# Eight PSUM banks in turn for the paired products, and a later rearrangement of the residual on GpSimd

## The reference

```
h2 = rmsnorm(x, norm2_g);  x = x + (silu(h2 @ w_gate) * (h2 @ w_up)) @ w_down      # first block,  1024 -> 2816 -> 1024
h2 = rmsnorm(x, g_ffn);    x = x + square(relu(h2 @ w_ff1)) @ w_ff2                # second block, 1024 -> 4096 -> 1024
```

## Time and profile before

| | |
|---|---|
| median of 3 runs | 2442.06 us (2441.98 to 2444.38) |
| the profiled execution | 2445.13 us, span 2443.2 us |
| TensorE busy | 2388.4 us (98%), 11414 matmuls |
| VectorE / ScalarE / GpSimd busy | 1864.7 (76%) / 1090.2 (45%) / 1155.4 (47%) us |
| mean granted TensorE clock | 0.991 |

### The profile page before, as it was taken

How to read it: one execution, slowest core, us unless ns; L and a number is a source line. 1 busy time by engine, 2 the same in 40 slices (tenths; PEclk the granted TensorE clock), 3 DMA queues, 4 the chain that set the end, 5 groups by cost and what they waited for, 6 DMA issues and landing times.

```text
span 2443.2 us, 31864 instructions
## 1 busy us (share of the span) xinstructions
PE 2388.4 (98%) x11414; PEld 1958.1 (80%) x11414; DVE 1864.7 (76%) x2405; ACT 1090.2 (45%) x1868; POOL 1155.4 (47%) x786
## 2 busy tenths in 40 slices
PE   9999999999999999999999999999999999999998
PEld 7777788888778888878877878887877888788876
DVE  6777767673687787789967966778288888999976
ACT  6454556562533333344435436555163333544423
POOL 4666651211555555554543463431256555554552
PEclk9999999999999999999999999999999999999999
DMA  4311321232122233363512772223223444654522
GB/s 161 81 48 52 92 61 36 60 122 70 52 65 78 88 115 103 104 200 119 181 54 105 179 163 61 61 59 109 76 81 108 146 148 160 228 168 148 180 80 101
DMA packets 228171, 263.06 MB, mean 108 GB/s; under 512 B 18224, under 2 KB 139824, under 8 KB 227888
## 3 DMA queue, kind: packets, MB, share of 16 engines
q1 hardware_dynamic: 224416, 248.72, 32.0%
q0 software_dynamic: 3168, 11.54, 2.5%
q10 hardware_dynamic: 432, 0.79, 0.1%
HBM read 169.74 MB, written 60.82 MB: 94 GB/s over the span
## 4 chain that ended last, share of the span: by engine, by line
PE 81%; DVE 9%; POOL 3%; ACT 3%; issue 3%; DMA 1%; SPq 0%; POOLq 0%; DVEq 0%; ACTq 0%
PE PS L1810 23%; PE PS L1815 23%; PE PS L1812 23%; PE PS L1908 3%; PE PS L1895 2%; PE PS L1929 2%; PE PS L1926 2%; PE PS L1889 2%; DVE R L2292 1%; DVE R L2222 1%; ACT R L2580 1%; DVE R L2252 1%; PE PS L1892 1%; DVE X L2300 1%; DVE Pb L2114 0%
## 5 line engine op out<-in xcount | busy, mean ns | idle before, releaser
L1810 PE MATMUL PS<-R,wh 128*128 128x512 f32 x2872 | 1139.3, 397 | 23.6 <-DVE mix L2203 6.3
L2670 POOL TENSOR_TENSOR lows<-values,wh 128x512 fp32r<-128x512 f32 (+1 forms) x486 | 718.3, 1484 | 903.7 <-ACT wh L2421 730.0
L1815 PE MATMUL PS<-R,wh 128*128 128x512 f32 x2872 | 1124.8, 392 | 2.6 <-DVE R L2248 1.9
L1812 PE MATMUL PS<-R,lows 128*128 128x512 f32 x2564 | 1002.7, 391 | 1.2 <-POOL lows L2670 1.2
L1810 PEld LDWEIGHTS PS<-R,wh 128*128 128x128 f32 x2872 | 542.5, 189 | 136.1 <-DVE mix L2203 7.6
L1815 PEld LDWEIGHTS PS<-R,wh 128*128 128x128 f32 x2872 | 541.3, 188 | 122.2 <-DVE R L2248 3.7
L1812 PEld LDWEIGHTS PS<-R,lows 128*128 128x128 f32 x2564 | 483.3, 189 | 96.0 <-issue 3.6
L2421 ACT ACTIVATE wh<-values 128x512 fp32r<-128x512 f32 (+2 forms) x487 | 301.9, 620 | 578.9 <-PE PS L1815 575.4
L2300 DVE TENSOR_TENSOR X<-PS,X 128x1024 f32<-128x1024 f32 x154 | 187.2, 1216 | 31.1 <-PE PS L1815 30.5
L2670 POOL TENSOR_TENSOR late_r<-late,wh 128x512 fp32r<-128x512 f32 x77 | 114.0, 1480 | 118.3 <-ACT wh L2421 56.3
L2537 ACT ACTIVATE PT<-PS 128x512 fp32r<-128x512 f32 (+1 forms) x200 | 108.2, 553 | 90.9 <-PE PS L1908 84.2
(11 more groups left out here) (279 smaller groups left out, 3027.9 us busy)
## 6 DMA issues: line engine op xcount, KB each, us to landing
scr_hid<-R1f SPq DMA_DIRECT2D x160, 256.0 KB, 3.0
values<-w_in_dram SPq DMA_DIRECT2D x88, 256.0 KB, 2.7
R1f<-scr_hid SPq DMA_DIRECT2D x88, 256.0 KB, 3.6
R0f<-scr_hid SPq DMA_DIRECT2D x86, 256.0 KB, 3.8
values<-w_ff_dram SPq DMA_DIRECT2D x60, 256.0 KB, 2.9
values<-w_ff_dram SPq DMA_DIRECT2D x100, 128.0 KB, 2.3
R<-R SPq DMA_DIRECT2D x96, 128.0 KB, 2.3
X<-X POOLq DMA_DIRECT2D x22, 512.0 KB, 5.8
```

Source lines behind the costliest of these rows:

```text
L1810: e.matmul(PS[:, b, :], wh, high, start=s["start"], stop=False, skip_group_check=on)
L1812: e.matmul(PS[:, b, :], wl, high, start=False, stop=False, skip_group_check=on)
L1815: m = e.matmul(PS[:, b, :], wh, low, start=False, stop=s["stop"], skip_group_check=on)
L2670: e.tensor_tensor(T.wl[piece.v][:, 0:m], T.wv[piece.v][:, 0:m], T.wh[:, piece.h, 0:m].bitcast(F), ALU.subtract).then_inc(*sg.up("w_lo", pi ...
```

## The change

Three things in the straight tiles and pairs. The straight tiles take all eight banks in turn. The pairs take the eight banks in the order of `SEVEN_BANKS`, which is 0, 1, 4, 5, 6, 7, 2, 3, starting at an index chosen so that the last product of the last pair is at the list's end. And `block_in` additionally waits for P4 of the pair before it in the list, the sixth and the eighth pair. A side effect: the line that set `dense_at` to 3 (n2) and 5 (n3) after the straight tiles is gone, so `dense_at` goes on from 8.

```
-            b = dict(P7=0, P4=1).get(name, self.seven_at % 3) if sums_late else self.seven_at % 3
+            b = SEVEN_BANKS[self.seven_at % 8]
...
-        O.dense_banks, O.dense_at = [2, 3, 0, 1], 0
+        O.dense_banks, O.dense_at = [2, 3, 0, 1, 4, 5, 6, 7], 0
...
-        O.dense_banks, O.dense_at = SEVEN_BANKS, -7 * len(factors) % 8
+        O.seven_at = -7 * len(factors) % 8
...
-                O.step("block_in", tag=tag, g=BLOCK_IN.index(i), given=whole)
+                O.step("block_in", tag=tag, g=BLOCK_IN.index(i), given=whole + [("dense", ((tag, i - 1), "P4"))])
```

## The result

| | before | changed |
|---|---|---|
| median | 2442.02 us (2441.25 to 2444.38, 4 runs) | 2413.01 us (2411.34 to 2416.88, 4 runs) |
| profiled execution, span | 2445.13, 2443.2 us | 2412.89, 2411.1 us |
| TensorE idle in the span | 54.8 us | 35.5 us |
| mean granted clock | 0.991 | 0.997 |

The ratio is 0.9882, 95% interval 0.9866 to 0.9897: 29.0 us faster. I had forecast 22.3 us and a range that ended at 2416.5. So the direction was right and the five places of my sum nearly so, and the size was too small by 6.7 us, outside the range.

A forecast was written before the change was run, and what follows sets the result against it. TensorE bounds the kernel, busy 2388.4 of 2443.2 us, so only its idling and clock loss can be won. Terms 8.4+0.8+3.0+0.6+4.7+3.5+1.3 = 22.3 us off 2442.06 give 2419.8, stated as 2420.0; range 2416.5 to 2428.

The forecast's parts named there:

- the five places of my sum: Gains: n2 start 8.4+0.8, n2 pairs' end 3.0, n3 start 0.6+4.7, n3 pairs' end 3.5, down projection 1.3 us.
- five clock stretches: At the seams: long stalls each bring a stretch at 1.2 GHz costing 1.7 us more; five fewer were expected.
- The coincidences of bank numbers: First pairs: with three banks, n2's pair 1 P1 stalls 0.79, n3's P7 3.04+1.7 clock; eight banks win 0.8+4.7.
- n3's P1: n3's first pair: P1 still takes the last straight half's bank; wait 0.9 in place of 1.52, 0.6 us won.
- The down projection: n3's direct tiles start at bank 6 instead of 3, where the last block's P5 just ended: 1.3 us won.
- The rearrangement costs nothing in the pairs: Behind P4 of the sixth and eighth pairs: cost 0, lows 1.2 us to spare; bounds 0 to +3.7 per place.
- The tiles between (projections with eight banks): Projections between the feed-forward stages and n3's direct tiles: banks turned by 5 of 8, gain nothing.
- a share returned: Pairs' ends: 3.6 (n2) and 4.2 (n3) won, 0.6 and 0.7 returned since VectorE's queue delays P6: 3.0 and 3.5.
- the first rival: Blocks after the pairs: they inherit the wait through VectorE's backlog, the 3.0 and 3.5 vanish, 2426.5 us; chance 0.10.
- The second: In the pairs: rearrangement makes lows or weight sums 2 us late at one to four places, +3.7 to +14.8; chance 0.12.
- The slower one: In the pairs: GpSimd waits for P4 a full product or more, lows late, 2441.8 to 2452.6 us; chance 0.03.
- The third: First pair: VectorE's own backlog, not banks, delays P6's right-hand sums, 9.2 us lost, 2429; chance 0.04.

The follow-up runs named there:

- e1: The kernel before with only the later rearrangement (block_in also waits for P4), banks as before: 2430.3 us against 2441.9.
- e8: The changed kernel with the pairs in three banks as before, the rest of the change in: 2425.8 us.
- e6: The kernel before with only dense_at set to 8 after the straight tiles in both stages: 2439.9 us against 2441.2.
- e10: The changed kernel with all four rearrangement instructions in one step behind P4 of the sixth pair: 2426.3 us.
- e5: The changed kernel with dense_at set to 3 and 5 after the straight tiles, as before: 2416.5 us.
- e9: The kernel of e5 with every engine's order planned for three pair banks and four straight-tile banks, late rearrangement in both plans: 2423.6 us.
- e3: The kernel before with eight banks for straight tiles and pairs, but engine orders planned for the old banks; rearrangement and dense_at as before: 2430.5 us.
- e2: The changed kernel without the later rearrangement, all bank edits in: 2421.95 us against 2441.9 for the kernel before.
- e12: The kernel before with eight planner passes in place of three, banks and rearrangement as before: 2432.5 us against 2443.1.

## Why the prediction was too small

**The step that failed.** My sum priced the waits next to the edited code and put everything else at nothing, as if each engine kept its order. It also gave back 0.6 and 0.7 us at the pairs' ends. In the profiled executions the places that I had at nothing gave 7.2 us, and nothing came back at the pairs' ends. TensorE's idle time fell by 19.3 us, where my sum has 13.8 (22.3 less five clock stretches, 8.5). The lower clock gave 12.8, where my sum has 8.5. For the whole change the mechanism at the five places was right, though at the pairs' ends and at n3's first seam the order has a share that I gave to the banks. What the sum lacked is the planner's new order and the clock stretches elsewhere. In the medians, where the clock's part is smaller, the miss is 6.7 us.

**Right, step by step.** GpSimd's rearrangement held VectorE at the n2 seam, and its move alone frees 8.5 us there (e1; 8.4 in my sum). The coincidences of bank numbers are gone with eight banks. With three, 0.78 is there in full, but the 3.04 has become 2.08 and 1.61 without a clock stretch (e1, e8), and 1.60 in e6, where the rearrangement stands at the seam. So a part of that term hung on the order. n3's P1 still waits, 0.79 (0.9 taken). The down projection gives 1.4 (1.3 taken). The rearrangement costs nothing in the pairs, with 1.3 us of cover left (1.2 taken; e10). Pairs still run at 226 ns a matmul.

**Point by point wrong.**

1. "The tiles between (projections with eight banks) are turned by 5 of 8: nothing" was wrong. Undoing it costs 3.5 us in the median (e5). 1.4 of them are the down projection, which I had. In the convolution and second attention 1.2 us of idle time come back, and the rest of the difference there is clock. That stretch also moves by 2.7 us between e5 and e9, which have the same banks in it, and is not won in e8, which has the turned banks. So the term was not nothing, but the turned banks are not shown to be its cause.
2. I took every row away from the edit as fixed. It isn't: one planner lays out all engines, and the new banks changed its limits. With the same banks and the same place of the rearrangement the order is worth 7.1 us (e9 against e5). In the traces it is 1.9 us at n2's pairs' end, 3.9 at n3's, 0.5 at n2's blocks' end, 1.7 at the last norm and 2.0 at the beginning (most of it one clock stretch), less the 2.7 that e9 wins in the convolution and second attention. So the terms that I took with a share returned (3.0 of 3.6, 3.5 of 4.2) came out whole, 3.8 and 4.4. The 0.8 at the last norm, where a stall of 1.38 us is gone, stood in no term.
3. In n2, at the blocks' end, I had index 3 before and after and no gain. The rows of the kernel before there and in n3's blocks:

```profile
1239.60 0.50 PE L1810 MATMUL PS<-R,wh 128*128 128x512 f32 x1 [1.77 <-DVE X L2300]
...
2200.08 0.50 PE L1810 MATMUL PS<-R,wh 128*128 128x512 f32 x1 [1.16 <-DVE X L2300]
```

The idle time went from 1.77 to 1.22, and the low-clock stretch behind it went too: 1.9 us. In e1 a stall of 1.76 at the same place came without that stretch, so 1.4 of the 1.9 is the clock's and not the change's. The 1.16 us in n3's blocks don't follow the banks either: they are gone in e1, e3, e5 and after, and there in e2 and e6 (1.06).
4. The bound. I put the lower end at "all lost time won" of the seams, less 2 us for scatter. With the planner re-laying the whole kernel, idle time and clock stretches anywhere are in play; e12 changes nothing but the order and moves 10.6 us. The upper end does not follow from its words: the first rival and one late place are 2426.5 + 3.7 = 2430.2, and I wrote 2428. That played no part in the miss.
5. I forecast five clock stretches fewer. The five at the seams are gone, but others went too, at n2's blocks' end and in the convolution and second attention, and how many come varies between runs of one kernel. So a part of the miss is luck.

**The rivals.** The first (blocks inherit the wait, 2426.5) needed the old order: e3 and e9 show it. The second had 1.3 us of cover against it, and no row at L1812 stands in the pairs. The slower one fell: GpSimd waited at most 0.8 us for P4 before a rearrangement, where it needed a full product. The third fell too: no idle row stands in the first pairs but the 0.79 before n3's P1, so VectorE's right-hand sums were done in time.

**The rule of the Trainium skill** (SBUF — State Buffer, Who interferes with whom): the hold is the same wherever the rearrangement stands, as the rule says, and the rows at 827 agree. What it can't say is whether anyone waits: at the seam TensorE did, in the pairs it didn't.

## What to carry to other kernels

Where a planner makes the order of all engines, an edit of one resource must be priced in two parts: the waits that it touches, read from the rows, and a free term for the re-laid order. Here that term was 7 us, and it can be measured by giving the old order to the new resources. Stretches at the lower clock belong in a term of their own, with a spread. Work that holds another engine up is best put where that engine has idle time and the consumer has cover, in pieces shorter than the cover: 5.1 us was free, 10.7 us in one piece cost 6.1 a time. More banks than three were worth nothing in the steady pairs; the gain was at seams, where the next stage's first buffers coincided with the last stage's last.

## What the runs showed of the hardware that I had not expected

The lower clock did not follow from the length of a stall alone. Windows of e1 (first two) and e2 (last) around three stalls of TensorE: 1.90 us at 1078 brought the mean clock to 0.83, 2.08 at 1859 and 2.10 at 1843 left it at 1.00:

```profile
1077.00:1087.00 10.00, 8.92 (x32) 7.24 (x33) 8.29 (x11) 5.25 (x10) 3.61 (x3) 0.83 0.87 284
1857.00:1867.00 10.00, 8.04 (x35) 6.68 (x36) 7.19 (x9) 3.66 (x6) 4.40 (x4) 1.00 0.17 50
```

```profile
1841.00:1851.00 10.00, 7.91 (x35) 6.56 (x36) 8.23 (x7) 4.06 (x7) 9.92 (x6) 1.00 0.40 138
```

The stall of 3.04 us at n3's first seam brought a stretch in the kernel before (0.83 in the earlier trace rows). In e12 it has the same length, at 1865.74, and none:

```profile
1863.00:1873.00 10.00, 7.25 (x32) 6.00 (x33) 7.98 (x10) 2.85 (x5) 4.14 (x4) 1.00 0.10 29
```

So the 1.7 us that I added to stalls above 1.8 is a price that some of them pay, not a term that each has; five stretches before and none after at the seams was as forecast.

GpSimd is slowed by VectorE as well. In the changed kernel the low parts with no SBUF-only instruction of VectorE beside them (under 5% of their time) take 1.31 us in the mean (119 of them), the others 1.46; in the kernel before 1.32 and 1.56. In e10 two of them take 1.27 at 842.10 and 843.33, while VectorE stands idle, and the two at 838.74 take 1.7 each, which made e10's low 0.4 us later than worked out. Their mean over the kernel fell from 1484 to 1414 ns with the change, though VectorE is busier; the cause was not looked into.
